# The norms between two layers: inputs split two tiles at a time, TensorE tile by tile over four output tiles, no weight work on GpSimd

## The reference

```python
mix = jnp.concatenate([rmsnorm(u, conv_out_norm[l]), rmsnorm(attn, attn_out_norm[l])], axis=-1) @ w_out[l]
x = x + rmsnorm(mix, post_mix_norm[l])
hf = rmsnorm(x, pre_ffn_norm[l])
ff = (jax.nn.silu(hf @ w_gate[l]) * (hf @ w_up[l])) @ w_down[l]
x = x + rmsnorm(ff, post_ffn_norm[l])
...
z = rmsnorm_2(h, norm1_g[l])
proj = z @ w_in[l]
```

## Time and profile before

| | us |
|---|---|
| median of 3 runs | 2878.29 (2877.2 to 2879.6) |
| the profiled execution | 2877.54 |
| its span, from the first to the last instruction | 2875.5 |
| TensorE busy | 1508.8 (52%) |
| VectorE busy | 2327.1 (81%) |
| ScalarE busy | 700.3 (24%) |
| GpSimd busy | 552.7 (19%) |

### The profile page before, as it was taken

The page is one execution under the profiler, slowest core; times in us unless marked ns, Lnnn a source line. Parts: engine busy times, 40 slices in busy tenths (PEclk is TensorE's granted clock), DMA queues, the critical chain, the costliest instruction groups (busy, mean ns, idle before and its releaser), DMA issues.

```text
span 2875.5 us, 26027 instructions
## 1 busy us (share of the span) xinstructions
PE 1508.8 (52%) x9198; PEld 1356.0 (47%) x9198; DVE 2327.1 (81%) x2801; ACT 700.3 (24%) x905; POOL 552.7 (19%) x619
## 2 busy tenths in 40 slices
PE   8998878999999999699984440000000000000000
PEld 8986767888888888698874440000000000000000
DVE  6974657665665566787669999999999999999998
ACT  5423544443444344446441110000000000000000
POOL 0000021000000000300003233443333333433331
PEclk9998889999999999899997765555555555555555
DMA  7543354555555555454558989999999999999997
GB/s 222 179 111 102 100 159 135 190 181 187 186 190 189 187 186 163 137 161 147 183 183 349 391 310 422 389 398 422 422 422 422 422 422 422 421 422 422 422 422 310
DMA packets 339313, 798.71 MB, mean 278 GB/s; under 512 B 23249, under 2 KB 270635, under 8 KB 273195
## 3 DMA queue, kind: packets, MB, share of 16 engines
q0 software_dynamic: 73728, 536.90, 45.2%
q1 hardware_dynamic: 265515, 260.96, 28.6%
HBM read 795.72 MB, written 2.10 MB: 277 GB/s over the span
## 4 chain that ended last, share of the span: by engine, by line
DVE 39%; issue 10%; PE 10%; ACT 1%; DMA 0%; POOL 0%; DVEq 0%; POOLq 0%
DVE pl L2031 10%; DVE pg L2031 10%; DVE row L2015 9%; PE pl L745 4%; PE pl L752 3%; DVE wlo L1507 1%; PE pl L748 1%; PE pl L749 1%; DMA row<-in_peer_u,expert 0%; DVE dots L2015 0%; DVE cand L1999 0%; DVE cand L1996 0%; DVE cposf L2002 0%; DVE x_split L1700 0%; DVE top_i L1966 0%
## 5 line engine op out<-in xcount | busy, mean ns | idle before, releaser
L1507 DVE TENSOR_TENSOR wlo<-raw,whi 128x1024 fp32r<-128x1024 f32 (+1 forms) x460 | 553.4, 1223 | 372.5 <-ACT whi L1067 369.8
L1067 ACT ACTIVATE whi<-raw 128x1024 fp32r<-128x1024 f32 (+1 forms) x468 | 479.0, 1041 | 519.1 <-PE pl L752 429.4
L745 PE MATMUL pl<-x_split,whi 128*128 128x512 f32 x1920 | 487.3, 396 | 26.0 <-DVE x_split L1700 18.0
L745 PEld LDWEIGHTS pl<-x_split,whi 128*128 128x128 f32 x1920 | 348.4, 191 | 91.1 <-issue 20.8
L752 PE MATMUL pl<-x_split,wlo 128*128 128x256 f32 x2720 | 382.9, 284 | 2.4 <-DVE wlo L1507 2.4
L752 PEld LDWEIGHTS pl<-x_split,wlo 128*128 128x128 f32 x2720 | 368.3, 192 | 21.9 <-DVE wlo L1507 2.8
L672 POOL DMA_INDIRECT row<-in_peer_u,expert x256 | 240.7, 940 | 485.1 <-DVE expert L2004 169.6
L672 POOL DMA_INDIRECT row<-in_peer_v,expert x256 | 243.3, 950 | 373.8 <-DVE dots L2015 184.0
L2031 DVE SCALAR_TENSOR_TENSOR pl<-row,dots,pl 128x2048 f32<-128x2048 f32 x127 | 299.0, 2354 | 13.9 <-DVE pl L2031 0.9
L2031 DVE SCALAR_TENSOR_TENSOR pg<-row,dots,pg 128x2048 f32<-128x2048 f32 x127 | 298.7, 2352 | 0.0
L2015 DVE CUSTOM_DVE_ANT_0 row<-row,pl 128x2048 f32<-128x2048 f32 x128 | 292.0, 2281 | 0.5
(11 more groups left out here) (293 smaller groups left out, 1665.4 us busy)
## 6 DMA issues: line engine op xcount, KB each, us to landing
raw<-in_w_in SPq DMA_DIRECT2D x50, 1024.0 KB, 5.4
raw<-in_w_gate SPq DMA_DIRECT2D x44, 1024.0 KB, 5.1
raw<-in_w_up SPq DMA_DIRECT2D x44, 1024.0 KB, 5.1
raw<-in_w_out SPq DMA_DIRECT2D x32, 1024.0 KB, 5.5
raw<-in_w_down SPq DMA_DIRECT2D x32, 1024.0 KB, 5.4
raw<-in_peer_wq SPq DMA_DIRECT2D x16, 1024.0 KB, 9.8
raw<-in_w_down SPq DMA_DIRECT2D x16, 768.0 KB, 4.8
raw<-in_w_ukv SPq DMA_DIRECT2D x4, 1024.0 KB, 5.4
```

The source lines that it names most:

```text
L745: mm(banks[f], w, xs[:, x].rearrange("p h s -> p (h s)"), start=first_product, stop=(half == 1 and t == k - 1), skip_group_check=True)
L1067: return nc.scalar.activation(o, i, ACT.Copy)
L1507: V.tensor_tensor(wlo[:, n % 4, 0:k, :], w[:, :, f, :], whi[:, n % 4, 0:k, :].bitcast(F32), ALU.subtract)\
```

## The change

- `residual` and `input_hi` work in eight steps of two tiles instead of four of four, and `x_hi` and `x_lo` count such steps (`SPLITS` holds the counts at which each layer begins).
- `two_groups` goes tile by tile over four pieces, that is four output tiles in four banks: for each input tile four products with `whi`; after the eight tiles of a half the four pieces' products with `wlo`. The second norm's sum stands in the second half, between the second and the third piece's `wlo` products.
- A new semaphore `hi_used` counts the halves' last `whi` product. ScalarE's `whi` copies for the second half wait for it (`after`), no longer for `piece_used`; VectorE's `wlo` there waits for `piece_used` (`early`).
- GpSimd writes no `wlo`. VectorE writes the first two pieces' ahead of the norm, the next two behind the fourth step.
- In all five norms of `wide_total` GpSimd adds only seven of eight pairs of squares; TensorE takes the last pair straight from ScalarE, with two more matmuls.

```diff
-POOL_LO = {"post": "gu0", "postf": "in2a"}
-SPLITS = {"in1": 0, "out1": 1, "ffn": 2, "in2": 3, "out2": 4}
+SPLITS = {"in1": 0, "out1": 4, "ffn": 8, "in2": 16, "out2": 24}
...
-                with pool.Fori(1, 4) as i:
+                with pool.Fori(1, 3) as i:
...
-                if name in POOL_LO:
-
-                    u, n = UNIT0[POOL_LO[name]], PIECE0[POOL_LO[name]]
-                    for q in range(4):
-                        w = raw[:, (u + q // 2) % RING, 0:KU * CG].rearrange("p (k f c) -> p k f c", k=KU, f=2)
-                        pool.wait_ge(w_hi, n + q + 1)
-                        nc.gpsimd.tensor_tensor(wlo[:, (n + q) % 4], w[:, :, q % 2, :], whi[:, (n + q) % 4].bitcast(F32),
-                                                ALU.subtract).then_inc(w_lo, 1)
+                pool.wait_ge(norm_sq, n + 7)
+                a = sq_r[:, 0] if sq is None else two_tiles(sq, 6)
+                nc.gpsimd.tensor_tensor(sq_sum[:], sq_sum[:], a, ALU.add).then_inc(sq_added, 1)
...
-                mm(pnorm, ones[:], sq_sum[:, 1, :], start=False, stop=True).then_inc(norm_sum, 1)
+                mm(pnorm, ones[:], sq_sum[:, 1, :], start=False, stop=False)
+
+                last = sq_r[:, 1] if name == "n2" else (tmp if name in ("ffn", "n1") else mix)[:, 14:16, :]
+                pe.wait_ge(norm_sq, sq_count(n, 7))
+                mm(pnorm, ones[:], last[:, 0, :], start=False, stop=False)
+                mm(pnorm, ones[:], last[:, 1, :], start=False, stop=True).then_inc(norm_sum, 1)
...
-                half_group(piece, 0, PAIRS[0], arriving=arriving, apart=apart)
-                half_group(piece + 2, 0, PAIRS[1], apart=apart)
-                norm()
-                half_group(piece + 4, 1, PAIRS[0], arriving=arriving, apart=apart)
-                half_group(piece + 6, 1, PAIRS[1], apart=apart)
+                for half in range(2):
+                    for t in range(KU):
+                        x = half * KU + t
+                        if t % 2 == 0:
+
+                            pe.wait_ge(x_lo, SPLITS[arriving] + x // 2 + 1)
+                        for q in range(4):
+                            n = piece + 4 * half + q
+                            if t == 0:
+                                pe.wait_ge(w_hi, n + 1)
...
+                    last.then_inc(hi_used, 1)
+                    for q in range(4):
+                        n = piece + 4 * half + q
+                        if half == 1 and q == 2:
+                            norm()
+                        pe.wait_ge(w_lo, n + 1)
...
-                        if n >= 4:
+                        if after:
+
+                            act.wait_ge(hi_used, after)
+                        elif n >= 4:
...
-                weights_hi(u + 2, pc + 4)
+                weights_hi(u + 2, pc + 4, after=None if c else 1)
...
-            in2_hi(1)
+            weights_hi(in2_unit(1), PIECE0["in2a"] + 4, after=3)
...
+                        if early:
+
+                            dve.wait_ge(piece_used, n - 3)
```

More of the change, by code:

```diff
@@ L1086, in norm_root, with weights_hi @@
                 activation(rstd[:], invms[:], ACT.Sqrt).then_inc(norm_rstd, 1)
-            def weights_hi(unit, piece, k=KU, i=None, step=0, halves=(0, 1)):
+            def weights_hi(unit, piece, k=KU, i=None, step=0, halves=(0, 1), after=None):
                 for half in halves:
@@ L1101, in input_hi @@
             def input_hi(ready, gain):
[L1103 to L1109 removed]
+                for t in range(0, DT, 2):
+                    act.wait_ge(ready, t // 2 + 1)
+                    activation(xhi[:, t, :], res[:, t, :], ACT.Copy, scale=col(gain, t))
+                    activation(xhi[:, t + 1, :], res[:, t + 1, :], ACT.Copy, scale=col(gain, t + 1)).then_inc(x_hi, 1)
+                    activation(tmp[:, t:t + 2, :], res[:, t:t + 2, :], ACT.Square).then_inc(norm_sq, 1)
             for t in range(TT):
@@ L1496, in norm_finish, with weights_lo @@
                         .then_inc(norm_out, 1)
-            def weights_lo(unit, piece, k=KU, i=None, step=0, between=None, halves=(0, 1)):
+            def weights_lo(unit, piece, k=KU, i=None, step=0, between=None, halves=(0, 1), early=False):
                 for half in halves:
```

58 lines of the change are left out of this document (26 added, 32 removed).

## The result

The changed kernel took 2893.19 us (median of 4 runs, 2892.23 to 2897.82), the kernel before 2877.74 beside it (4 runs, 2877.03 to 2879.60): a ratio of 1.0056, with a 95% interval of 1.0038 to 1.0073. The profiled execution has a span of 2890.8 us against 2875.5. The forecast was 2891, slower, with a range of 2880 to 2898.

A forecast was written before the change was run, and what follows sets the result against it. TensorE was taken to set the pace until about 1500 us, so delays at A and B reach the end. 2.4 + 2.3 + 8.0 + 0.8 = 13.5 over the median 2878.29, forecast 2891; range 2880 to 2898, once given from 2885.

The forecast's parts named there:

- A: Place of the norms between the first out projection and the gates, about 414 to 467 us; net +2.4 us without restarts.
- B: Place of the norms between down projection and second block's in projection, about 1187 to 1244 us; net +2.3 without restarts.
- rstd to last square: Residual at A and B in steps of two tiles: 26.5 us from VectorE having rstd to ScalarE's last square.
- first restart: At A and B, TensorE idles before the second half and resumes at low clock; 2.0 us each.
- second restart: At A and B, TensorE waits after its last low products and resumes at low clock; 2.0 us each.
- n2: A later norm whose sum gets two more matmuls while TensorE is late there; +0.8 us, from 0.7 to 2.1.
- The tail: After the last square at A and B: TensorE needs the fourth whi copy, and the norm sum stands behind most products.
- four cold restarts: Two waits each at A and B drop TensorE's clock; 2.0 us each, +8.0 in all, ends 0 and 9.6.
- Rival 1: No cold restarts: idle stretches near 3.5 to 4.6 us might leave the clock up; 2884 us, chance 0.12.
- Rival 3: Cycling over four banks keeps the clock low in the second half at A and B; 2900 us, chance 0.05.
- The adds: In the residual each GpSimd add costs VectorE 1.05 us; six before the eighth add make 6.3.
- Rival 2: GpSimd's adds block nothing, so the residual is much shorter and the change faster; 2875 or 2871 us, chance 0.10.

The follow-up runs named there:

- adds_left_out: Changed kernel with GpSimd's six adds of squares left out at ffn and n1, so the output differs; 2880.87 us, ratio 1.0011.
- sum_early: Changed kernel with the second norm's sum moved back between the halves, products still tile by tile; 2882.85 us, ratio 1.0022.
- second_half_by_piece: As sum_early, but the second half goes piece by piece as before and only the first half tile by tile; 2868.36 us, ratio 0.9973.
- clock_held: lambda_early with small matmuls of the ones, into a bank nobody reads, in the places where TensorE waits; 2877.93 us, ratio 1.0005.
- old_order_fine_steps: Changed kernel with TensorE's whole order as before and copies on `piece_used`; VectorE, ScalarE and GpSimd as changed; 2865.78 us, ratio 0.9965.
- lambda_early: Changed kernel with VectorE's small operations on lambda moved ahead of the second norm's root at B; 2888.34 us, ratio 1.0043.

## Why the prediction was right

The direction, the mechanism and the chief terms hold. By the steps of the sum, in us:

| step | predicted | measured |
|---|---|---|
| rstd earlier at A, B | 0.54, 2.17 | 0.51, 2.24 |
| rstd to last square | 26.5 | 27.09, 27.11 |
| last square to sum read, A, B (with the first restart of 2.0) | 16.1, 17.6 | 16.4, 17.8 |
| of which the first restart | 2.0, 2.0 | 1.9, 1.5 |
| sum read to next group, A | 6.3 | 6.3 |
| second restart, A, B | 2.0, 2.0 | 2.7, 2.2 |
| clock at the start of the down projection | not in the sum | 1.0 |
| n2 | 0.8 | 1.7, 0.4 ahead of it, less 0.9 behind it |
| sum | 13.5 | 17.5 |

The second restart at B is what remains of the 7.2 us lost there when the other rows are taken off.

- **Until rstd and the residual.** Both right to some tenths. The residual is 0.6 longer at each place, and not by the adds: without them it took 20.75 us, where the same terms make 20.2. A pair of scalings and the add behind it take 1.52 us from start to start (425.64 to 427.16 in adds_left_out), where the sum had 1.45, eight times over. The terms 16.4, 2.3 and 6.3 also make 25.0, not 25.1.
- **The tail.** Both reasons given, the fourth copy and the sum behind the products, are shown by sum_early and second_half_by_piece. A third that I had not named, that the gate's own output tile is finished late, was hidden behind the late sum and set sum_early's time. Without the restarts A lost 3.4 and B 3.5 us, where the sum had 2.4 and 2.3: 0.6 and 0.5 of it in the residual, 0.3 and 0.7 in the tail.
- **The clock.** That four cold restarts come, and where, is shown by clock_held. Their sum is right, 8.3 against 8.0, though single ones lie between 1.5 and 2.7: I took the row's low window and halved it, which gives what is lost inside it. The second restart at A cost 2.7 in the first two pieces (5.07 and 3.17 against 2.79 each). What I had at nothing is the clock in the unchanged part: at the start of the down projection it fell in the changed kernel and not in the kernel before, which is 1.0 us of the difference. Rival 1 is out. Rival 3 is out: PEclk is 0.98 in the middle of the products that cycle over four banks, here in the changed kernel.

```profile
455.00:459.00 4.00, 4.00 (x19) 3.31 (x18) 0.00 (x0) 0.00 (x0) 0.00 (x0) 0.98 0.78 246
```

The Trainium skill, "TensorE: Matmul & The Clock Gate", section "A second HAM failure mode: psum-queue depth-cycling", describes that failure for another kernel; no run here shows it where the inputs were all there.
- **The adds.** 1.06 us of an add that takes 1.3. The Trainium skill, "SBUF — State Buffer", section "SBUF: two separate sides", has one side holding the shared ports for its whole instruction while the other waits. The trace agrees in that one VectorE operation is stretched for each add; the price, a quarter of a microsecond under the add's recorded length, is the measured one.
- **Rival 2** had the right question: whoever takes the adds off VectorE's path gains. But the fine steps alone don't, and adds_left_out, at 2880.87, is still not faster than the kernel before, because the tail is untouched.
- **n2** was mis-sized by 0.9 in place (four matmuls at low clock from 1498.66 to the reading at 1502.45, 3.79 us, against 2.08); 0.4 more were lost between B and it, and 0.9 given back behind it.
- **The figures of the forecast.** 2878.29 + 13.5 = 2891.8 rounds to 2892, not 2891. The text gives the range once from 2885 and once from 2880; the measured time lies in both. The sign "next group at about 473" counts a restart that only comes behind that start; the sum's own terms give 471, and it started at 469.80, with E 2.1 earlier.

The terms together were 4.0 us short: 1.0 at A and 1.2 at B without the restarts, 0.3 in the restarts, 1.0 at the down projection and 0.4 around n2. That the profiled execution came out only 1.8 above the forecast difference (15.3 against 13.5) is owed to E, which fell 2.1 us earlier in this execution by chance, and no merit of the sum.

## What to carry to other kernels

An order of products that lets the inputs in earlier finishes every output later; before taking it, look at who waits for the first finished output and for any buffer that all of them share, and use it only for the stretch in which inputs are late (here the first half, where even then it brought nothing: 0.1 us or less at either place). Take a helper's adds away from where they hold up the engine that sets the pace, and give them to an engine at a time in which it waits for that very data; not to one that is itself late. Where executions scatter ahead of the change, measure from a milestone just before it as well: then the same kernel repeated within 0.2 us here, the medians within some 3. And before a difference of one or two microseconds is put down to the change, look whether it arises where the change is: here up to 3.1 us came and went with the clock in stretches that all runs share.

## What the runs showed of the hardware that was not expected

**The clock can fall without a long wait.** In sum_early TensorE came to the second half at full clock, ran one product a microsecond for 2.75 us behind the copies, and the granted clock fell in the dense stretch behind it. Windows of that run:

```profile
450.48:451.30 0.82, 0.46 (x2) 0.15 (x1) 0.82 (x1) 0.82 (x2) 0.00 (x0) 1.00 0.00 0
451.30:452.30 1.00, 0.51 (x2) 0.20 (x2) 1.00 (x2) 1.00 (x2) 0.00 (x0) 1.00 0.00 0
452.30:453.20 0.90, 0.48 (x1) 0.17 (x1) 0.90 (x2) 0.88 (x1) 0.00 (x0) 1.00 0.00 0
453.20:456.40 3.20, 3.17 (x9) 2.55 (x10) 3.17 (x4) 0.00 (x0) 0.00 (x0) 0.65 0.78 249
```

No single wait there was longer than 0.45 us (the last before it, for the last squares, was 0.82). clock_held put small matmuls between such products too, but what these do without the ones in the long waits was not run.

**The same wait, and another clock.** At the start of the down projection TensorE waits 2.02 or 2.03 us for `whi` in all fourteen profiles. In eight the clock then fell, in six it did not. The changed kernel and old_order_fine_steps, which run the same instructions there; the granted clock was 0.50 from 1131.77 to 1134 us in the first and 1.00 from 1121.65 to 1124 in the second:

```profile
1129.77 1.86 PE L743 MATMUL pl<-h_split,whi 128*128 128x512 f32 x6 [2.02 <-ACT whi L1086]
1132.72 2.36 PE L743 MATMUL pl<-h_split,whi 128*128 128x512 f32 x6
```

```profile
1119.65 1.65 PE L743 MATMUL pl<-h_split,whi 128*128 128x512 f32 x6 [2.03 <-ACT whi L1064]
1121.84 1.54 PE L743 MATMUL pl<-h_split,whi 128*128 128x512 f32 x6
```

From the start of VectorE's last `hid<-silu,pl` to the last square of "postf" it took 70.6 us in all eight, 69.0 in four of the six and 69.6 in two (the kernel before and clock_held); for these 0.6 us I have no cause. In the pooling of the second block, behind a wait of 2.01 to 2.04 us, the same happens: the eight matmuls there took 2.39 to 3.32 us in nine profiles and 1.96 or 1.97 in five, which is again 1.6 us to the sum of n2 (168.3 us in the changed kernel against 166.7 in lambda_early, from VectorE's product `l_i` near 1330 us to the reading of that sum). For the two kernels that were profiled twice the clock fell at the same of these spots both times. What decides it, these runs don't show. It means that the length of a wait near 2 us does not tell whether the clock falls.

**Repeatability.** Behind E the two executions of the changed kernel agree within 0.2 us to the end, and the kernel before within 0.2 as well, though its stretch between the places took 723.2 and 722.6; E itself moves by 5.1 in the changed kernel. Nearly all scatter of one kernel that I saw arises in its first 415 us; what makes it was not tried.
